# Expert stages: the branch condition turned round, the gathered part first, the part for all tokens behind

## The reference, cut to what matters

```python
gate = g_w * softmax(top_v)                       # two weights per token
expert = g_idx * EXPERTS_PER_GROUP + top_i        # two of 32 experts per token
hid = silu(xblk @ w_gate[e]) * (xblk @ w_up[e])   # 1024 -> 512, the rows of expert e
y   = hid @ w_down[e]                             # 512 -> 1024
out = zeros_like(h).at[row_tok].add(y * row_w)    # back to the tokens
```

## Time and profile before

| What | Value |
|---|---|
| median of 3 runs | 1908.77 us (1908.24 to 1909.62) |
| profiled execution, its own time | 1911.03 us |
| its span, first to last instruction | 1909.2 us |
| mean granted TensorE clock | 0.989 |
| PE busy | 1846.7 us, 97% |
| DVE busy | 570.2 us, 30% |
| ACT busy | 361.9 us, 19% |
| DMA | 592.14 MB, mean 310 GB/s |
| instructions in the trace | 22702 |

### The profile page before, as it was taken

The page is one execution under the profiler, slowest core; times in us unless marked ns, Lnnn a source line. Parts: engine busy times, 40 slices in busy tenths (PEclk is TensorE's granted clock), DMA queues, the critical chain, the costliest instruction groups (busy, mean ns, idle before and its releaser), DMA issues.

```text
span 1909.2 us, 22702 instructions
## 1 busy us (share of the span) xinstructions
PE 1846.7 (97%) x9434; PEld 1195.2 (63%) x9434; DVE 570.2 (30%) x1288; ACT 361.9 (19%) x809; POOL 13.6 (1%) x28
## 2 busy tenths in 40 slices
PE   8999999999999999999999988999999999988998
PEld 7798888957988888575444433335885444433334
DVE  3279550432655703533111110112233111110112
ACT  3440000322301003433211111112013211111111
POOL 1000000000001000000000000000000000000000
PEclk9999999999999999999999999999999999999998
DMA  9746676432377762229999999999557999999995
GB/s 301 271 177 247 273 304 255 188 132 89 133 290 294 300 239 89 89 113 368 432 431 430 429 431 433 430 427 428 215 208 277 430 431 430 430 431 433 430 427 240
DMA packets 45485, 592.14 MB, mean 310 GB/s; under 512 B 5698, under 2 KB 14282, under 8 KB 17106
## 3 DMA queue, kind: packets, MB, share of 16 engines
q1 hardware_dynamic: 44818, 588.74, 74.9%
q10 hardware_dynamic: 576, 2.10, 0.3%
HBM read 585.34 MB, written 1.05 MB: 307 GB/s over the span
## 4 chain that ended last, share of the span: by engine, by line
PE 80%; DMA 17%; DVE 1%; ACT 1%; issue 0%; DVEq 0%; SPq 0%; ACTq 0%
PE ps L540 27%; PE ps L1241 18%; DMA ring<-in_w_up 17%; PE ps L781 8%; PE ps L1357 7%; PE ps L1212 3%; PE ps L1205 2%; PE ps L610 2%; PE ps L827 1%; PE ps L699 1%; PE ps L628 1%; PE ps L642 1%; PE ps L988 1%; PE ps L1416 1%; PE ps L1028 1%; PE ps L595 1%
## 5 line engine op out<-in xcount | busy, mean ns | idle before, releaser
L540 PE MATMUL ps<-hsq,ring 128*128 128x256 f32 x2048 | 447.3, 380 | 0.8 <-DVE hsq L2064 0.8
L1241 PE MATMUL ps<-ring,work 128*64 128x512 f32 x1792 | 408.7, 610 | 39.4 <-DMA ring<-in_w_up 30.7
L540 PEld LDWEIGHTS ps<-hsq,ring 128*128 128x128 f32 x2048 | 387.8, 190 | 59.5 <-issue 7.0
L1241 PEld LDWEIGHTS ps<-ring,work 128*64 128x64 f32 x1792 | 129.3, 140 | 308.7 <-issue 249.7
L1631 ACT ACTIVATE work<-ps 128x512 f32<-128x512 f32 (+2 forms) x175 | 89.6, 516 | 828.6 <-PE ps L540 325.1
L1357 PE MATMUL ps<-ring,work 128*64 128x512 f32 x896 | 198.4, 595 | 1.1 <-DVE work L2557 1.1
L781 PE MATMUL ps<-work,ring 128*128 128x256 f32 (+1 forms) x704 | 148.5, 373 | 0.0
L2009 DVE SCALAR_TENSOR_TENSOR work<-ring,silu_c,work 128x512 f32<-128x512 f32 x196 | 143.7, 754 | 5.1
L781 PEld LDWEIGHTS ps<-work,ring 128*128 128x128 f32 x704 | 130.5, 190 | 18.7 <-issue 1.7
L1357 PEld LDWEIGHTS ps<-ring,work 128*64 128x64 f32 x896 | 61.9, 137 | 120.9 <-issue 118.0
L2512 DVE TENSOR_TENSOR work<-ps,work 128x512 f32<-128x512 f32 x26 | 18.0, 692 | 392.1 <-ACT work L1631 392.1
(11 more groups left out here) (324 smaller groups left out, 1357.5 us busy)
## 6 DMA issues: line engine op xcount, KB each, us to landing
ring<-in_w_gate SPq DMA_DIRECT2D x20, 4096.0 KB, 21.4
ring<-in_w_up SPq DMA_DIRECT2D x20, 4096.0 KB, 20.4
ring<-in_w_down SPq DMA_DIRECT2D x18, 4096.0 KB, 20.4
ring<-in_w_ada SPq DMA_DIRECT2D x24, 2048.0 KB, 8.8
ring<-in_w_down SPq DMA_DIRECT2D x20, 2048.0 KB, 16.3
ring<-in_w_gate SPq DMA_DIRECT2D x16, 2048.0 KB, 16.2
ring<-in_w_up SPq DMA_DIRECT2D x14, 2048.0 KB, 19.0
ring<-in_w_ff_gate SPq DMA_DIRECT2D x10, 2048.0 KB, 13.7
```

Source lines behind the costliest of these rows:

```text
L540: last = mm(ps[:, b, 0:T], w[:, k, m * P:(m + 1) * P], rhs[:, k, :], start=(i == 0), stop=(i == nk - 1))
L1241: last = mm(ps[e * CAP:(e + 1) * CAP, w, :], xg[:, k, e * CAP:(e + 1) * CAP], tile_of(first, w, i, 2 * k // KT, e, k % HTL), start=(k == 0 ...
```

## The change

On each of the four engines the condition is turned from `most > CAP` to `most <= CAP`, and the two bodies change places. The instructions of either body stay as they were. The diff on three engines, ACT's moved lines cut:

```diff
@@ PE
-                with pe.If(most > CAP):
+                with pe.If(most <= CAP):
+                    gathered_tokens(e_, first)
+                with pe.Else():
                     all_tokens(e_, first)
-                with pe.Else():
-                    gathered_tokens(e_, first)
@@ SP
-                with sp.If(most > CAP):
+                with sp.If(most <= CAP):
+                    pairs_of_gathered_tokens()
+                with sp.Else():
                     pairs_of_all_tokens()
-                with sp.Else():
-                    pairs_of_gathered_tokens()
@@ ACT
-                with act.If(most > CAP):
-                    act.wait_ge(e_["row_full"], 1)
...
-                with act.Else():
+                with act.If(most <= CAP):
                     def gate_out(i):
...
+                with act.Else():
+                    act.wait_ge(e_["row_full"], 1)
...
@@ DVE
-                with dve.If(most > CAP):
+                with dve.If(most <= CAP):
+                    gathered_tokens(e_)
+                with dve.Else():
                     all_tokens(e_, l)
-                with dve.Else():
-                    gathered_tokens(e_)
```

More of the change, by code:

```diff
@@ L1974, in experts @@
                     rows_out(NEXP // 2 - 1)
+                with act.Else():
+                    act.wait_ge(e_["row_full"], 1)
+                    A(root[:], ps[:, 2, 0:T], ACT.Sqrt, bias=eps[:], scale=1.0 / D).then_inc(e_["all_root"], 1)
+                    with act.Fori(0, NEXP // 2) as i:
+                        for e in range(2):
+                            act.wait_ge(e_["row_full"], 2 * i + e + 2)
+                            A(gb[:, e, :], ps[:, 3, 0:T], ACT.Copy).then_inc(e_["row_copied"], 1)
+                            for m in range(HTL):
+                                act.wait_ge(e_["gate_full"], 8 * i + 4 * e + m + 1)
+                                A(esg[:, m % 2, :], ps[:, 2 * (m % 2), 0:T], ACT.Sigmoid).then_inc(e_["gate_sig"], 1)
+                    A(small[:, 62:63], eps[:], ACT.Copy).then_inc(S["sorted_in"], 2 * BLOCKS)
                 if l:
```

## The result

The changed kernel took 1912.57 us (median of 20 runs, 1908.32 to 1914.35), the kernel before on the same chip 1909.09 us (20 runs, 1906.52 to 1911.08). The ratio is 1.0018, with a 95% interval of 1.0012 to 1.0024: by the medians 3.5 us slower, by the interval 2.3 to 4.6 us. The ratios here are worked out from the single runs, so they are not exactly the quotient of the two medians. The forecast was 1908.8 us, with a range from 1907.3 to 1912.5.

The account below looks back on a forecast made before the run. The prediction took PE to bound the kernel, with 80% of the chain of waits (DMA 17%). Its terms, 0 at the start, 0 at the end and 0 on the other engines, gave 1908.8 us, range 1907.3 to 1912.5.

Parts of the forecast that it names:

- The start: PE's far jump at the start of the part goes away; already hidden behind queued matmuls, so gain 0.
- The other engines: End jumps on ACT, DVE and SP: 0.05 to 0.07 us as at the start, value 0.
- The arrival at the end jump: PE's sequencer meets the jump behind the last `down` at 1315.5 in layer 0, 1889.4 in layer 1.
- The cover: Queued matmuls of the last `down` keep PE busy until 1319.30 in layer 0, from the jump met at 1315.5.
- the end jump's price of 3.46 us: PE's far jump behind the last `down`: 3.46 us per layer, hidden, value 0; upper bound without cover 6.9 us.
- the 0.3 us to spare: End of layer 0: jump left at 1319.0, PE has work until 1319.30; each 0.1 us beyond costs 0.1 us.
- one of the prediction's own signs of being wrong: Idle time before L1212, or another listed gap, of over 2 us per layer would make the forecast wrong.
- none for the next 6 us: After the start jump at 879.3 one instruction packet loads at once, a second only within 887.9 to 889.2.
- The second packet that is waited for: Rival: behind the end jump the sequencer stalls again, 3.2 us over two layers; chance 0.16 including a later arrival.
- ACT as the missing engine: Rival: ACT's end jump held 3.4 us, together 4.6 us, 1913.4; ACT or PE fully exposed, chance 0.05.
- A gain at the start: Rival: PE's sequencer 3.4 us earlier helps weights or clock; at most 6.8 us, 1902.0; faster, chance 0.05.
- The jump that costs 3.4 us whether taken or not: Rival: L1191's conditional branch on PE keeps 3.4 us, the end is free, time 1908.8; chance 0.04.

Follow-up runs that it names:

- e1: Changed kernel with PE's branch put back to its old order, ACT, DVE and SP still turned; 1909.16 us, ratio 1.0000 to the kernel before.
- e2: Kernel before with PE's branch alone turned round; 1913.71 us, ratio 1.0016.
- e5: Kernel before with PE's branch turned round in layer 0 alone; 1911.88 us, ratio 1.0009.
- e4: Changed kernel with two more 2 MB loads, read by nobody, in 16 KB packets in layer 1; 1915.82 us, ratio 1.0032 to the kernel before.
- e8: Kernel before with PE waiting at the end of layer 0 for five POOL fills of an unread tile; 1913.47 us, ratio 1.0017.
- e6: Kernel before with PE's branch turned round in layer 1 alone; 1909.64 us, ratio 1.0001.
- e7: Changed kernel with two more unread 2 MB loads in layer 1, each in four pieces (4 KB packets); 1916.40 us, ratio 1.0031 to the kernel before.

## Why the prediction was wrong

**What held.** The start: the far branch is gone, and PE was busy 25.50 of 25.50 us, so its removal brought nothing. The other engines: 0.04 to 0.06 us each, and e1 gives 1.0000. The arrival at the end jump: forecast 1315.5 in layer 0 from the landing of the last `down` half; in the changed kernel it landed at 1289.9 + 24.3 = 1314.2, as this row of its issue has it, and the jump was met at 1314.3:

```profile
L1490 SPq DMA_DIRECT2D ring<-in_w_down x2: 327/328/328, 1286.5 to 1289.9; - x2
...
DMA to landing us min/median/max: 22.8/23.6/24.3
```

The cover: forecast 3.8 us, measured 1318.33 - 1314.3 = 4.0 us. And layer 1: hidden, 3.31 us against 1894.08 - 1890.0 = 4.1 us.

**What failed.** One term of the sum was mis-sized: the end jump's price of 3.46 us in layer 0, taken "since engine and distance are the same". The prediction took the same figure as the upper bound of that price. It was 6.22 us, and so the 0.3 us to spare in layer 0 became a gap of over 2 us, one of the prediction's own signs of being wrong. Engine and distance were the same, the DMA engines were not: the instruction packet on q8 started 3.7 us behind the jump, behind a stretch where the data queue filled all 16 engines, as these rows of the changed kernel from 1314.3 to 1317.9 and, for q8, from there to 1318.1 show:

```profile
q1 hardware_dynamic: 105, 1.52, 100.3%
q14 instruction: 1, 0.01, 0.6%
...
q8 instruction: 1, 0.02, 31.8%
```

The smaller packet on q14 is not what the jump waits for: the profiles of e2 and e5 have none from the jump to the q8 packet, and their jumps take 6.21 and 6.27 us. The prediction had passed over such a packet as well: its "none for the next 6 us" behind the first jump is true of q8 alone, as the earlier trace rows has one on q14 there.

In layer 1 of the changed kernel nothing but the q8 packet moves from the jump at 1890.0 to 1891.1 (it starts 1.0 us behind the jump):

```profile
q8 instruction: 1, 0.02, 5.3%
```

The trace of before held the hint. The prediction never asked what data the DMA engines were moving behind the old jump; the share of 0.99 over 25.5 us looks like full load. But in the microsecond behind it, 879.3 to 880.3, the data queue was running empty (and in layer 1, from 1452.6 to 1453.6, no packet at all was under way):

```profile
q1 hardware_dynamic: 49, 0.29, 68.5%
```

So 3.46 us was a calm price, applied to the one place where the next layer's weights are already streaming. With 6.22 us the prediction's own steps give 6.22 - 3.8 = 2.4 us of idle time, and 2.37 was measured. That they meet so closely is in part luck: the cover was 4.0 us, and the first matmul started 0.2 us behind the jump's end, and these two cancel.

**What was not in the sum.** The granted clock behind the gap. Of eight gaps of 2.07 to 2.40 us before `add_rows`, in the profiles of the changed kernel and of five experiments, six were followed by the half clock, and the rows behind them came 1.5 to 1.7 us later; two (the changed kernel, and e4 in layer 0) were not. My estimate from these: 2.37 + 6/8 x 1.65 = 3.6 us, against 3.5 us measured. The share of 6/8 rests on eight gaps in six profiles only. The mean granted clock of the timed runs points to less: e2 has 0.9899 against 0.9903 for the kernel before, e8 0.9902 against 0.9907, e5 0.9908 against 0.9907. Over 1910 us that is an estimated 0.8 and 0.9 us and nothing, each uncertain by about as much, where 6/8 x 1.65 is 1.2 us. So the gap is shown, and the clock's share of the 3.5 us is not settled.

The trace of before could have put this term into the sum. Its two gathered parts have twelve idle times of PE of 2.20 to 2.63 us before an L1241 row, with weights as the releaser, and the half clock follows eight of them. Here is one of these gaps, then PE's busy time behind it, and then PE's busy time behind a gap of 2.20 us, with the full clock:

```profile
1101.09 8.57 PE L1241 MATMUL ps<-ring,work 128*64 128x512 f32 x32 [2.63 <-DMA ring<-in_w_up]
...
1101.20:1104.10 2.90, 2.90 (x8) 0.50 0.94 407
...
1159.40:1162.80 3.40, 3.40 (x16) 1.00 1.03 443
```

The length alone does not decide it: in the changed kernel's profile, gaps of 2.61 and 2.63 us before L1241 rows kept the full clock too.

**The rivals.** The second packet that is waited for gave 1912.0, near the time measured, by a mechanism that the trace refutes. The second packet comes at 1324.2, 9.9 us behind the jump and 3.7 us behind its end, and PE's L1416 row runs through there unbroken; in layer 1 nothing is lost either. ACT as the missing engine: 0.04 us, refuted. A gain at the start: none. The jump that costs 3.4 us whether taken or not: refuted by 0.095 and 0.079 us at the start.

**A rule beside it.** The instruction packet began about 1.0 us behind the jump in calm stretches and 3.7 us in layer 0 under load, 2.7 us more, which is nearly all of the 2.8 us that the jump took more. The Trainium skill, in "DMA: Bandwidth & Descriptors", section "Queues, rings and completion order", says that each DMA engine takes its queue rows in turn, a whole packet at a time. It counts several descriptors to a packet, about 9 to 17. By that rule, if the packet of the rule were the packet that the trace records, the wait should shrink with the packets' size. Here it hardly did: 6.23 us with 16 KB and 5.97 us with 4 KB. Either the two packets are not the same, or something ahead of the engines holds the fetch; no run here decides it.

**What stays open.** Whether the fetch waits for a fixed amount of data or a fixed time; why two of the eight gaps kept the full clock, and how much the clock adds in the median; and why the instruction packet itself is slower at times. The last is most of why e1's start branches are 3.8 and 4.1 us long, against 3.46 and 3.36 before (hidden in both): their packets start 1.0 us behind the branch as before, but take 1.5 and 1.7 us, not 1.1. This is the q8 packet's share of the 16 engines in the 3 us behind the branch of layer 1, in e1 and then before; the data queue's share there is 57.5% and 57.4%:

```profile
q8 instruction: 1, 0.02, 3.5%
...
q8 instruction: 1, 0.02, 2.2%
```

No version tried beats the kernel before; e1 and e6 equal it.

## What to carry to other kernels

Price a far jump on PE with the DMA traffic of the microsecond behind it, not with a share averaged over a stage. Put it where the DMA is calm, since the queued work covered only some 4 us here and not the 6 us of a jump under load, and leave it where it is already hidden. And when a cover is worked out to within 0.3 us, take as the range's upper end the price of the disputed step under the worst traffic, plus the slower clock that such a gap may bring. Look in the trace of before for gaps of the same length: it may show how often that happens.

## What the runs showed of the hardware

- A jump over 2172 matmuls on PE took 3.3 to 4.1 us where the data queue was empty or running empty behind it, and 5.9 to 6.3 us with the weight stream at full rate (13 and 7 jumps in ten profiles); a near one 0.07 to 0.10 us. On ACT, DVE and SP all took 0.04 to 0.07 us.
- The instruction packet started 0.9 to 1.2 us behind the jump in calm stretches, 3.4 to 3.7 us under load, and there with 16 KB and with 4 KB data packets alike (3.7 and 3.5 us in layer 1 of e4 and e7).
- An idle time of PE of only 2.1 to 2.4 us before `add_rows` was followed by the half clock in six of eight cases, and the rows behind came 1.5 to 1.7 us later each time. In the trace of before, eight of twelve idle times of 2.2 to 2.6 us were followed by it.
